# Second branch's decay-weighted attention (four 128-token tiles) rewritten as a chunkwise recurrence with a carried state

## What is computed

```python
b = jnp.cumsum(lf, axis=-1)
D = jnp.where(causal, b[..., :, None] - b[..., None, :] + li[..., None, :], -jnp.inf)
m_inter = b + m[..., None]
m_t = jnp.maximum(m_inter, jnp.max(D, axis=-1))
w_inter = jnp.exp(m_inter - m_t)
P = jnp.exp(D - m_t[..., None])
s_qk = jnp.einsum('bhtd,bhsd->bhts', qc, kc) * P
num = w_inter[..., None] * einsum('bhtd,bhde->bhte', qc, C) + einsum('bhts,bhse->bhte', s_qk, vc)
den = w_inter * einsum('bhtd,bhd->bht', qc, n) + jnp.sum(s_qk, axis=-1)
h = num / jnp.maximum(jnp.abs(den), jnp.exp(-m_t))[..., None]
```

## Time and profile before

| | us |
|---|---|
| median of 3 runs (511.46 to 511.62) | 511.49 |
| the profiled execution | 511.43 |
| its span | 509.7 |
| PE busy | 500.9 (98%) |
| PE weight loads busy | 411.4 (81%) |
| DVE / ACT / POOL busy | 258.7 / 236.1 / 214.6 |
| share of PE in the chain that ended last | 94% |

### The profile page before, as it was taken

How to read it: one execution, slowest core, us unless ns; L and a number is a source line. 1 busy time by engine, 2 the same in 40 slices (tenths; PEclk the granted TensorE clock), 3 DMA queues, 4 the chain that set the end, 5 groups by cost and what they waited for, 6 DMA issues and landing times.

```text
span 509.7 us, 6792 instructions
## 1 busy us (share of the span) xinstructions
PE 500.9 (98%) x2506; PEld 411.4 (81%) x2506; DVE 258.7 (51%) x568; ACT 236.1 (46%) x417; POOL 214.6 (42%) x142
## 2 busy tenths in 40 slices
PE   8999999999999999999999999999999999999995
PEld 7688888888888878888777877888888888887885
DVE  3875778877999915515555557551110011125433
ACT  6756754655533443464577563333321333142322
POOL 1675231333344453256487433056435653373000
PEclk9999999999999999999999999999999999999999
DMA  8653531222243432112121121142244326444111
GB/s 285 200 140 121 140 96 53 84 83 53 74 123 83 120 108 83 42 43 83 44 81 46 47 76 42 42 123 73 56 121 123 107 59 206 125 134 155 41 52 74
DMA packets 44842, 48.94 MB, mean 96 GB/s; under 512 B 4997, under 2 KB 30213, under 8 KB 44809
## 3 DMA queue, kind: packets, MB, share of 16 engines
q1 hardware_dynamic: 43944, 47.65, 32.0%
q10 hardware_dynamic: 864, 0.86, 0.5%
HBM read 46.40 MB, written 2.11 MB: 95 GB/s over the span
## 4 chain that ended last, share of the span: by engine, by line
PE 94%; DMA 2%; SPq 1%; POOL 1%; ACT 1%; DVE 1%; issue 1%; DVEq 0%
PE pj L1423 24%; PE pj L1425 23%; PE pj L1424 23%; PE ob L1533 2%; PE tr L1524 2%; DMA w_raw<-in_w_in 2%; PE ob L1504 2%; PE qb L1494 2%; PE qb L1489 2%; PE qb L1488 2%; PE ob L1424 1%; PE qb L1424 1%; PE ob L1425 1%; PE qb L1425 1%; PE ob L1423 1%; PE qb L1423 1%
## 5 line engine op out<-in xcount | busy, mean ns | idle before, releaser
L513 POOL TENSOR_TENSOR w_lo<-w_raw,w_hi 128x1024 fp32r<-128x1024 f32 x70 | 168.8, 2421 | 144.5 <-ACT w_hi L856 144.4
L1423 PE MATMUL pj<-w_hi,h_hi 128*128 128x512 f32 x272 | 112.8, 415 | 0.0
L1425 PE MATMUL pj<-w_hi,h_lo 128*128 128x512 f32 x272 | 106.5, 392 | 0.0
L1424 PE MATMUL pj<-w_lo,h_hi 128*128 128x512 f32 x272 | 106.5, 391 | 0.0
L1423 PE MATMUL pj<-h_hi,w_hi 128*128 128x512 f32 (+1 forms) x200 | 78.1, 390 | 1.0 <-DVE h_lo L1086 1.0
L856 ACT ACTIVATE w_hi<-w_raw 128x1024 fp32r<-128x1024 f32 (+1 forms) x72 | 73.5, 1045 | 10.2 <-DMA w_raw<-in_w_out 6.4
L1425 PE MATMUL pj<-h_hi,w_lo 128*128 128x512 f32 (+1 forms) x200 | 77.9, 389 | 0.0
L1424 PE MATMUL pj<-h_lo,w_hi 128*128 128x512 f32 (+1 forms) x200 | 77.9, 389 | 0.0
L1425 PEld LDWEIGHTS pj<-w_hi,h_lo 128*128 128x128 f32 x272 | 51.0, 188 | 11.4
L1423 PEld LDWEIGHTS pj<-w_hi,h_hi 128*128 128x128 f32 x272 | 51.2, 188 | 9.7 <-issue 1.1
L1424 PEld LDWEIGHTS pj<-w_lo,h_hi 128*128 128x128 f32 x272 | 51.3, 188 | 9.4 <-issue 1.0
(11 more groups left out here) (201 smaller groups left out, 817.6 us busy)
## 6 DMA issues: line engine op xcount, KB each, us to landing
w_raw<-in_w_in SPq DMA_DIRECT2D x60, 512.0 KB, 3.6
w_raw<-in_w_out SPq DMA_DIRECT2D x5, 512.0 KB, 3.7
x_tok<-in_x SPq DMA_DIRECT2D x4, 512.0 KB, 5.0
w_raw<-in_w_branch_a SPq DMA_DIRECT2D x8, 256.0 KB, 3.0
w_raw<-in_w_branch_b SPq DMA_DIRECT2D x8, 256.0 KB, 3.3
x_again<-in_x SPq DMA_DIRECT2D x1, 2048.0 KB, 10.4
w_late<-in_w_out SPq DMA_DIRECT2D x3, 512.0 KB, 7.3
out<-y_norm SPq DMA_DIRECT2D x4, 320.0 KB, 2.5
```

Source lines behind the costliest of these rows:

```text
L513: eng.tensor_tensor(lo[:, 0:m], raw_slot(n)[:, 0:m], hi[:, 0:m].bitcast(F32), ALU.subtract).then_inc(lo_by_dve if n in DVE_SLOTS else lo_b ...
L1423: pe.matmul(bank, a_hi, b_hi, start=first, stop=False)
L1424: pe.matmul(bank, a_hi, b_lo, start=False, stop=False)
L1425: return pe.matmul(bank, a_lo, b_hi, start=False, stop=last)
```

## The change

The second branch goes over to chunks of 128 tokens. Within a chunk the masked product stays as it was. What comes from earlier chunks is taken from a state of 128x129 numbers per head: keys of chunk c are transposed to token by channel and scaled per token, multiplied with the chunk's values, and added to the decayed state; queries scaled per token are multiplied with the state. Blocks between distant chunks are gone.

```diff
@@ plan()
-        put(p, "qk_b", h, 0)
-        put(p + 1, "qk_b", h, 1)
-        put(p + 2, "qk_b", h, 2)
-        put(p + 3, "qk_b", h, 3)
-        for i in range(TILES):
-            put(p + 4 + i, "pv_b", h, i)
+        put(p, "kt_b", h)
+        put(p, "qk_b", h)
+        put(p + 2, "state_b", h)
+        put(p + 3, "pv_b", h, 0)
+        put(p + 5, "pv_b", h, 1)
+    put(first["bv"] + 2, "scales_in")
+    put(first["bv"] + 6, "scales")
...
@@ GpSimd, side(p)
-                    wait_full(pool, ("qk_b", B_HEADS - 1, TILES - 1))
+                    wait_full(pool, ("pv_b", B_HEADS - 1, 1))
...
-                        d = decay[:, e % 2, 0:P]
+                        d = decay[:, h % 2, :].rearrange("p (c t) -> p c t", t=P)
                         pool.affine_select(out=d, in_=d, compare_op=ALU.is_ge, fill=0.0, base=0,
-                                           pattern=[[1, P]], channel_multiplier=-1).then_inc(decay_cut, 1)
+                                           pattern=[[0, TILES], [1, P]], channel_multiplier=-1).then_inc(decay_cut, 1)
@@ ScalarE, job_side(job)
-                    act.activation(decay[:, e % 2, 0:SEQ - j * P], neg_m_all[:, h, j * P:SEQ], ACT.Exp,
-                                   bias=gate_tok[:, 0, j, h:h + 1]).then_inc(decay_made, 1)
+                    for j in range(TILES):
+                        t = slice(j * P, (j + 1) * P)
+                        ins = act.activation(decay[:, h % 2, t], neg_m_all[:, h, t], ACT.Exp,
+                                             bias=gate_tok[:, 0, j, h:h + 1])
+                    ins.then_inc(decay_made, 1)
...
+                    for j in range(1, TILES):
+                        ins = act.activation(e_row[:, h % 2, (j - 1) * P:j * P], neg_m_all[:, h, j * P:(j + 1) * P],
+                                             ACT.Exp, bias=m_end[:, j - 1, h:h + 1])
+                    ins.then_inc(e_row_made, 1)
+                elif kind == "scales":
+                    act.wait_ge(chunk_w_in, 1)
+                    act.activation(chunk_w[:, :, :], chunk_w[:, :, :], ACT.Exp).then_inc(chunk_w_made, 1)
+                elif kind == "kt_b":
+                    wait_full(act, job)
...
+                    for c in range(TILES - 1):
+                        ins = act.activation(k_tok[:, h % 2, c, :], bank_of(job)[:, c * P:(c + 1) * P], ACT.Copy,
+                                             scale=chunk_w[:, c, h:h + 1])
+                    ins.then_inc(k_tok_made, 1)
@@ ScalarE, split_queries(i)
-                    wait_full(act, ("qk_b", B_HEADS - 1, TILES - 1))
+                    wait_full(act, ("pv_b", B_HEADS - 1, 1))
@@ VectorE, job_side(job)
+                    dve.scalar_tensor_tensor(out=sp[:, h % 2, :], in0=bank_of(job)[:, :], scalar=float(B_DIM) ** -0.5,
+                                             in1=decay[:, h % 2, :], op0=ALU.mult, op1=ALU.mult).then_inc(sp_made, 1)
+                    dve.wait_ge(e_row_made, h + 1)
+                    dve.scalar_tensor_tensor(out=q_e[:, h % 2, :], in0=qk_b[:, h, P:SEQ], scalar=float(B_DIM) ** -0.5,
+                                             in1=e_row[:, h % 2, :], op0=ALU.mult, op1=ALU.mult).then_inc(q_e_made, 1)
+                elif kind == "scales_in":
...
+                    dve.tensor_scalar(m_end[:, :, :], ends[:, 0:n, :], -1.0, None, ALU.mult)
+                    dve.tensor_tensor(chunk_w[:, 0:n, :], gate_tok[:, 0, 0:n, :], ends[:, 0:n, :], ALU.add)
+                    dve.tensor_tensor(chunk_w[:, n:2 * n - 1, :], ends[:, 1:n, :], ends[:, 0:n - 1, :], ALU.subtract)\
+                        .then_inc(chunk_w_in, 1)
+                elif kind == "state_b":
+                    wait_full(dve, job)
...
+                    link(dve.tensor_copy(state[:, h % 2, 0, :], kv[:, 0, :]))
+                    for c in range(1, TILES - 1):
+                        ins = dve.scalar_tensor_tensor(out=state[:, h % 2, c, :], in0=state[:, h % 2, c - 1, :],
+                                                       scalar=chunk_w[:, TILES - 2 + c, h:h + 1], in1=kv[:, c, :],
+                                                       op0=ALU.mult, op1=ALU.add)
+                        if c < TILES - 2:
+                            link(ins)
+                    ins.then_inc(state_made, 1)
@@ TensorE, side(job)
+                elif kind == "kt_b":
+                    for c in range(TILES - 1):
+                        ins = pe.transpose(bank[:, t], qk_b[:, B_HEADS + h, t], ident[:, :])
+                elif kind == "qk_b":
+                    for c in range(TILES):
+                        ins = pe.matmul(bank[:, t], qk_b[:, B_HEADS + h, t], qk_b[:, h, t], start=True, stop=True)
+                elif kind == "state_b":
+                    wait_read(pe, ("kt_b", h))
...
+                    for c in range(TILES - 1):
+                        ins = pe.matmul(bank[:, c * (B_DIM + 1):(c + 1) * (B_DIM + 1)], k_tok[:, h % 2, c, :],
+                                        v_b[:, c, h, :], start=True, stop=True)
+                elif kind == "pv_b":
+                    wait_read(pe, ("qk_b", h))
+                    wait_read(pe, ("state_b", h))
+                    pe.wait_ge(q_e_made, h + 1)
+                    for c in (2 * g, 2 * g + 1):
+                        ins = pe.matmul(bank[:, cols], sp[:, h % 2, c * P:(c + 1) * P], v_b[:, c, h, :],
+                                        start=True, stop=(c == 0))
+                        if c:
+                            ins = pe.matmul(bank[:, cols], q_e[:, h % 2, (c - 1) * P:c * P], state[:, h % 2, c - 1, :],
+                                            start=False, stop=True)
```

More of the change, by code:

```diff
@@ L165 @@
            "probs_chan": "tr", "out_a_chan": "tr", "out_b_chan": "tr",
-           "score": "q", "qk_b": "q", "qk_a": "q", "pv_b": "o", "pv_a": "o"}
+           "score": "q", "qk_b": "q", "qk_a": "q", "pv_b": "o", "pv_a": "o", "kt_b": "tr", "state_b": "o"}
+NOT_PE = ("scales_in", "scales")
 def fills():
@@ L173, in fills @@
     bank, before, order = {}, {}, {}
-    for job in [job for p in sorted(SIDE) for job in SIDE[p]] + [LAST_SIDE]:
+    for job in [job for p in sorted(SIDE) for job in SIDE[p] if job[0] not in NOT_PE] + [LAST_SIDE]:
         order[job] = len(order)
@@ L305, in hybrid_kernel @@
         ik_lo = at("ik_lo", [P, SEQ], F32R, z_a + 12288)
-        PACKED = P * TILES * (TILES + 1) // 2
-        sp = at("sp", [P, 2, PACKED], F32, z_a)
-        decay = at("decay", [P, 2, SEQ], F32, z_a + 10240)
+        sp = at("sp", [P, 2, SEQ], F32, z_a)
+        k_tok = at("k_tok", [P, 2, TILES - 1, P], F32, z_a + 4096)
+        state = at("state", [P, 2, TILES - 1, B_DIM + 1], F32, z_a + 7168)
+        decay = at("decay", [P, 2, SEQ], F32, z_a + 10272)
+        q_e = at("q_e", [P, 2, SEQ - P], F32, z_a + 14368)
+        e_row = at("e_row", [P, 2, SEQ - P], F32, z_h)
         norm_b_row = at("norm_b_row", [P, WIDTH], F32, z_norm_b)
@@ L1223, in job_side @@
                 elif kind == "qk_b":
-                    h, j = job[1:]
-                    e = h * TILES + j
-                    w = SEQ - j * P
+                    h = job[1]
                     wait_full(dve, job)
[L1228 to L1233, removed]
+                    dve.wait_ge(decay_cut, h + 1)
@@ L1285, in cell_scale @@
             def cell_scale():
[L1287 removed]
+                wait_read(dve, ("pv_b", B_HEADS - 1, 1))
                 dve.wait_ge(en_made, 1)
@@ L1489, in side @@
                     ins = pe.matmul(bank[:, 0:w], queries, ik_lo[:, 0:w], start=False, stop=True)
-                elif kind == "qk_b":
[L1491 to L1499, removed]
+                elif kind == "kt_b":
+                    h = job[1]
+                    if h == 0:
+                        pe.wait_ge(qk_b_ready, 2 * B_HEADS)
+                    for c in range(TILES - 1):
+                        t = slice(c * P, (c + 1) * P)
+                        ins = pe.transpose(bank[:, t], qk_b[:, B_HEADS + h, t], ident[:, :])
+                elif kind == "qk_b":
+                    h = job[1]
+                    for c in range(TILES):
+                        t = slice(c * P, (c + 1) * P)
+                        ins = pe.matmul(bank[:, t], qk_b[:, B_HEADS + h, t], qk_b[:, h, t], start=True, stop=True)
+                elif kind == "state_b":
+                    h = job[1]
+                    wait_read(pe, ("kt_b", h))
+                    if h == 0:
@@ L1500, in side @@
                         pe.wait_ge(v_ones_made, 1)
                         pe.wait_ge(relu_used, len(SCORES))
[L1502 to L1505, removed]
+                    for c in range(TILES - 1):
+                        ins = pe.matmul(bank[:, c * (B_DIM + 1):(c + 1) * (B_DIM + 1)], k_tok[:, h % 2, c, :],
+                                        v_b[:, c, h, :], start=True, stop=True)
+                elif kind == "pv_b":
+                    h, g = job[1:]
+                    wait_read(pe, ("qk_b", h))
```

(6 more changed lines are left out.)

60 lines of the change are left out of this document (43 added, 17 removed).

## The result

The changed kernel takes 513.88 us (median of 4 runs, 513.83 to 514.93); the kernel before, measured beside it, takes 511.56 (4 runs, 511.46 to 511.62). The ratio is 1.005, 95% interval 1.0038 to 1.0063: slower by 2.3 us, where the prediction had 0.5 us faster and at most 512.6. The profiled execution of the changed kernel took 513.84 us, its span is 512.1.

What follows compares the result with a forecast made beforehand. The prediction took TensorE, busy throughout branch B, as the bound. Work removed 17.60 us less added 13.64 gives 3.96, less waits of 3.46 gives 0.50; 511.49 - 0.50 = 511.0 us, range 509.9 to 512.6.

Steps and rivals of the forecast that it cites:

- TensorE's work in branch B: Branch B's four heads on TensorE: 17.60 us of work removed, 13.64 us added, a gross gain of 3.96 us.
- Waits: New TensorE waits before `pv_b`: head 0 1.93 us, head 1 1.03, heads 2 and 3 0.1 each, 3.46 with weight loads.
- the round in front of the state: VectorE's top-128 search round of place 109, 2.22 us, runs before head 0's state; head 1 has its round there too.
- The reload: After a wait TensorE must load weights before its product: 0.15 us for each of heads 0 and 1, bounds 0 and 0.2.
- The mask: GpSimd's mask in branch B, now over 512 columns, takes 0.62 us, bounds 0.27 and 1.06.
- The rival of the expensive mask: GpSimd's mask over four blocks costs more than its columns; at 1.43 us the time is 512.6 us; chance 0.11.
- Net of branch B: Branch B's gross gain of 3.96 us less TensorE's waits of 3.46 us leaves 0.50 us faster.
- The good bounds together: Mask of 0.27 us (+0.7) with no reload and no tie (+0.5): the gain reaches 1.6 us.
- After place 128 TensorE is as dense as before, so the gain is carried to the end.: Behind branch B TensorE loses nothing, so the 0.50 us gain stays whole to the kernel's end.
- The clock rival: Head 0's wait drops TensorE to 1.2 GHz; 3.0 us there cost 1.5 us, time 512.5 us; chance 0.04.
- Smaller waits: Branch B's mask takes 0.40 us, with no reload and no tie: gain 1.4 us, time 510.1; chance 0.22.
- no waits: TensorE never waits in branch B, place 109's round not standing before the state: gain 3.96 us, time 507.5; chance 0.05.

Runs made afterwards that it cites:

- rounds_around: Changed kernel with all old tiles at their old addresses, VectorE's top-128 rounds 12 and 13 at place 107, 14 at 115, 15 at 122: 508.37 us.
- same_addr: Changed kernel with its two new small tiles laid over two not yet in use, constants' zone back at 3328 bytes, old addresses restored: 511.37 us.
- shift192: Kernel before with only its constants' zone grown from 3328 to 3520 bytes, moving every tile behind by 192; no instruction changed: 514.16 us.
- f_only: Kernel before with 192 bytes put before zone f, so only tiles from there on move (`oa`, `iq_parts` among them): 512.87 us.
- pad64: Kernel before with its constants' zone grown by 64 bytes to 3392, all tiles behind moved by 64: 513.33 us.
- pad256: Changed kernel with its constants' zone at 3584 bytes, so tiles behind move by 256 instead of 192 against the kernel before: 511.51 us.

## Why the prediction was wrong, point by point

- **TensorE's work in branch B**: right in kind, a little small. By distances of starts less 0.23: transposes with scores 1.23 us a head (forecast 1.21), `state_b` 0.67 (0.66), the second `pv_b` 0.89 (0.88), the first 0.74 (0.66). That makes 14.1 us instead of 13.64, a gross gain of 3.5 instead of 3.96.
- **Waits**: head 0 2.01 us against 1.93 + 0.15, head 1 1.08 against 1.03 + 0.15, heads 2 and 3 0.14 each against 0.1; in sum 3.37 against 3.46. Their cause is the round in front of the state, as argued: with it gone `rounds_around` gains 3.2 us. The reload that I priced at 0.15 is at most the 0.10 us between the state's end and the product.
- **The mask** took 0.64 us against 0.62, ScalarE's ten short instructions 2.92 us from the first start to the last end, 0.29 each against 0.30. The rival of the expensive mask is refuted.
- **Net of branch B**: 3.5 - 3.4 = 0.1 by these terms, 0.23 by the starts, 0.50 forecast. (The good bounds together come to 0.50 + 0.7 + 0.5 = 1.7, not 1.6; the range would have begun at 509.8, which changes nothing.) With the old addresses (`same_addr`) this part alone lies inside the range.
- **The step that failed** is "After place 128 TensorE is as dense as before, so the gain is carried to the end." It is as dense by its busy share and less dense by its passes: 499 instead of 505 in the gate stage's window, 151 instead of 154 in the output stage's. The term missing from the sum is +2.6 us, measured alone by `shift192`; some 0.65 of it arise even before 121 us, in the part ahead of branch B, which the sum did not name at all. I had the two lines of the zone before me and gave them no cost, and so no rival: no case of mine had a mechanism outside branch B. Sum with it: -0.2 + 2.6 = +2.4, measured +2.3.
- **The clock rival** (0.04) was far too small a chance. Its mechanism is real: about 3.4 us at half rate cost 1.4 us (the long runs of `same_addr` against the others), near the 1.5 I gave it. With 6 of 20 runs, five of them by their time alone, at a rest of 1.85 us it is not the median, so it did not decide; in the changed kernel one of four runs, 514.93, is 1.1 us above the others, which fits, but it was not profiled.
- **Smaller waits, no waits**: neither happened; the waits were as forecast.

## What to carry to other kernels

Where memory is laid out by hand, look at what an edit does to the addresses behind it: here 192 bytes of new constants cost TensorE 2.6 us, more than the rewritten attention gave back as it was placed, and padding to 256 cost nothing. A shortened chain is worth only what the engine that makes its last link has free: put long work that nobody waits for (here the search's rounds) away from in front of it. And compare passes per window, not busy shares, when a full engine may have become slower.

## What the runs showed of the hardware that I had not expected

- A pass of 512 columns in fp32r comes every 0.226 to 0.227 us in the late stages when the zone of its operands starts where the old layout had it or 256 bytes on, and every 0.229 to 0.233 on the average of a stage when one of them is off by 64, 128 or 192, at a granted clock of 1.00. Passes whose own operands did not move can slow down too, by 0.001 to 0.002 us (`ob` in `f_only`, `h` in `pad64`). The 256-column passes at the end of the output stage, which read the same moved `m`, do not show it (the lag goes from +2.47 to +2.44 there). What in the chip does this is not settled; the runs show only the remainder of the shift.
- TensorE's clock fell behind a rest of 1.85 us in the profiled execution of `pad256` and stayed at 1.00 behind the same rest in that of `same_addr`. By time and mean clock it falls in some executions of one kernel and not in others, and in all four after 4.1 us.
- A running GpSimd instruction can hold a VectorE one until it ends itself (191.58 against 191.36 above). Not every one is held: the `MATCH_REPLACE8` at 188.91, beside the same remainder for most of its time, took 0.54 us as elsewhere. The holding is seen a second time, in VectorE's order of time, before and after:

```profile
233.32 0.17 DVE L1290 TENSOR_TENSOR den<-den,en_m 128x16 f32<-128x16 f32 x1
```

```profile
233.67 1.32 DVE L1350 TENSOR_TENSOR den<-den,en_m 128x16 f32<-128x16 f32 x1
```

A maximum over 16 columns, with two inputs in SBUF, takes 1.32 us instead of 0.17, as it now falls beside GpSimd's split queries, which end at 234.96 where it ends at 234.99. It costs nothing here: TensorE does not wait in that part.
